# Moving two weight splits behind the last evacuations of the up-projection

## The reference, cut to what matters

```python
def conv_glu_ffn(h, w_up, conv_w, conv_b, w_down, rows):
    up = h @ w_up
    a, v = up[..., :D_FF], up[..., D_FF:]
    if rows is None:
        a = dwconv1d_centred(a, conv_w[FFN_CONV // 2])
    else:
        a = dwconv2d_grid(a, conv_w, rows)
    return (jax.nn.silu(a + conv_b) * v) @ w_down
```

## Time and profile before

| | us |
|---|---|
| median of three runs | 1760.85 |
| the profiled execution's own time | 1758.34 |
| its span | 1756.5 |
| PE busy in the span | 1613.1 |
| POOL busy | 909.2 |
| DVE busy | 900.9 |
| ACT busy | 709.4 |

### The profile page before, as it was taken

One profiled execution on the slowest core, in us unless ns is written; L12 is line 12 of the kernel. 1 busy time (PEld: TensorE's weight loads), 2 busy tenths in 40 slices (PEclk: granted clock), 3 DMA queues, 4 the chain that ended last, 5 costly groups with the idle time before them and its releaser, 6 DMA issues.

```text
span 1756.5 us, 31356 instructions
## 1 busy us (share of the span) xinstructions
PE 1613.1 (92%) x11787; PEld 1486.6 (85%) x11787; DVE 900.9 (51%) x1751; ACT 709.4 (40%) x1174; POOL 909.2 (52%) x516
## 2 busy tenths in 40 slices
PE   4999999999988999998799999988987969999995
PEld 2999987766977999997699899878787949999994
DVE  1533105655337777523733355778754256777423
ACT  2554432333324444333546453544434344444322
POOL 1455556566643555554345455777552524555551
PEclk9999999999998999999899999899878979999998
DMA  8334336786322333432223221000012313334320
GB/s 321 106 109 132 123 118 247 289 288 223 120 96 72 120 131 121 143 130 73 96 96 109 96 97 63 23 14 25 14 50 96 120 60 100 127 127 133 132 99 36
DMA packets 54967, 205.24 MB, mean 117 GB/s; under 512 B 6096, under 2 KB 6096, under 8 KB 54352
## 3 DMA queue, kind: packets, MB, share of 16 engines
q1 hardware_dynamic: 54864, 203.80, 34.1%
HBM read 196.44 MB, written 7.34 MB: 116 GB/s over the span
## 4 chain that ended last, share of the span: by engine, by line
PE 51%; issue 23%; POOL 12%; DVE 7%; DMA 4%; ACT 2%; POOLq 0%; SPq 0%; DVEq 0%; ACTq 0%
POOL wlo L287 12%; PE ps L325 5%; PE ps L327 5%; PE ps L326 5%; DMA raw<-w_ada_in 4%; PE ps L2308 4%; PE ps L2310 4%; PE ps L2309 4%; PE ps L770 3%; PE ps L772 3%; PE ps L771 3%; PE ps L367 1%; PE ps L1531 1%; PE ps L1429 1%; PE ps L1074 1%
## 5 line engine op out<-in xcount | busy, mean ns | idle before, releaser
L287 POOL TENSOR_TENSOR wlo<-raw,whi 128x1024 fp32r<-128x1024 f32 (+1 forms) x201 | 511.5, 2546 | 494.7 <-ACT whi L277 494.7
L277 ACT ACTIVATE whi<-raw 128x1024 fp32r<-128x1024 f32 (+1 forms) x250 | 274.9, 1101 | 600.5 <-PE ps L327 373.0
L325 PE MATMUL ps<-hhi,whi 128*128 128x384 f32 x704 | 239.1, 340 | 24.9 <-DVE hlo L432 24.9
L326 PE MATMUL ps<-hlo,whi 128*128 128x384 f32 x704 | 237.2, 337 | 0.0
L327 PE MATMUL ps<-hhi,wlo 128*128 128x384 f32 x704 | 237.1, 337 | 0.0
L609 DVE SCALAR_TENSOR_TENSOR evac<-ps,vec,evac 128x189 f32<-128x189 f32 (+3 forms) x440 | 166.6, 412 | 101.6 <-ACT evac L560 72.0
L2104 POOL TENSOR_TENSOR wlo<-raw,whi 128x1024 fp32r<-128x1024 f32 x49 | 118.2, 2412 | 143.8 <-ACT whi L277 143.8
L542 DVE SCALAR_TENSOR_TENSOR xr<-xr,evac 128x384 f32 x32 | 64.2, 2006 | 192.7 <-ACT evac L511 191.5
L325 PEld LDWEIGHTS ps<-hhi,whi 128*128 128x128 f32 x704 | 133.2, 189 | 30.7 <-issue 29.3
L2308 PE MATMUL ps<-hhi,whi 128*128 128x384 f32 x392 | 142.1, 363 | 13.0 <-DVE hlo L432 12.3
L770 PE MATMUL ps<-hhi,whi 128*128 128x384 f32 x392 | 133.3, 340 | 10.6 <-DVE hlo L432 10.0
(11 more groups left out here) (297 smaller groups left out, 3362.1 us busy)
## 6 DMA issues: line engine op xcount, KB each, us to landing
raw<-w_in_in SPq DMA_DIRECT2D x98, 512.0 KB, 3.5
raw<-w_ada_in SPq DMA_DIRECT2D x96, 512.0 KB, 5.1
raw<-w_up_in SPq DMA_DIRECT2D x88, 512.0 KB, 3.4
raw<-w_down_in SPq DMA_DIRECT2D x32, 704.0 KB, 4.1
raw<-w_out_in SPq DMA_DIRECT2D x32, 512.0 KB, 3.5
s<-s_ssd_in SPq DMA_DIRECT2D x8, 256.0 KB, 5.6
o_ssd_out<-st_sb SPq DMA_DIRECT2D x8, 256.0 KB, 2.7
S<-s_gdn_in SPq DMA_DIRECT2D x4, 512.0 KB, 3.4
```

Of the source, the lines that this page charges most:

```text
L277: act.activation(whi[:, s.mod(SPL), 0:p.kt * P], raw[:, b.mod(RAW), 0:p.kt * P], ACT.Copy).then_inc(hi_ready, 1)
L287: pool.tensor_tensor(wlo[:, s.mod(SPL), 0:p.kt * P], raw[:, b.mod(RAW), 0:p.kt * P], whi[:, s.mod(SPL), 0:p.kt * P].bitcast(F32), ALU.subt ...
L325: pe.matmul(out, a, rhi[:, r, :], start=(r == 0), stop=False)
L326: pe.matmul(out, a, rlo[:, lo_tile(r) if lo_tile else r, :], start=False, stop=False)
```

## The change

The two `split_hi` calls for the down-projection leave the last two steps of `up_act`. `up_act` now evacuates all 44 blocks and writes the last `hidden_hi`; only then `split_first` splits down blocks 0 and 1. It is called for both layers, so the change stands at two places of the program.

```diff
-            staggered(act, p, lambda j: split_hi(act, p, j), [(0, 1, tile_centre), (1, 2, silu), (2, p.n - 2, evacuate)])
-            for k in range(2):
-                split_hi(act, phase[f"down{lay}"], Idx(k))
-                evacuate(Idx(p.n - 2 + k))
+            staggered(act, p, lambda j: split_hi(act, p, j), [(0, 1, tile_centre), (1, 2, silu), (2, p.n, evacuate)])
             hidden_hi(Idx(FF_T - 1))
 
         def up_dve(dve, lay):
@@
                 modulate_hi(act, 2 * lay + 1)
                 up_act(act, lay)
+                split_first(act, f"down{lay}")
                 back_act(act, f"down{lay}", 2 * lay + 1)
```

## The result

Five runs of the changed kernel took 1771.06 to 1778.74 us, median 1773.51, against a median of 1760.06 us (1758.14 to 1765.07, five runs) of the kernel before. These two medians differ by 13.5 us. There are 27 runs of the changed kernel in all, 1771.06 to 1781.75 us, median 1775.9, which is 15.8 above 1760.06. The ratio of the two kernels is given as 1.0088, 95% interval 1.0073 to 1.0103: 15.5 us slower (12.8 to 18.2). Forecast were 17.5 us.

What follows compares the result with a forecast made beforehand. PE was taken as the bound of the down-projection, with nothing behind its first matmul to absorb delay. Relay 6.25 plus clock 2.5 gave 8.75 us a place, 17.5 for two; 1760.85 + 17.5 = 1778, range 1770 to 1784 us.

Steps and rivals of the forecast that it cites:

- The first split was covered by PE's last up block: Up-to-down passage, before the change: nearly the whole 1.38 us split of down block 0 lies under PE's up block 43.
- The relay: Up-to-down passage: tile 21's chain, then split, POOL and PE, starts the first down matmul 6.25 us later per place.
- The low part of tile 20 at 0.56: DVE, between taps and product: takes 0.56 us instead of 3.41, because POOL is idle until the moved split is done.
- The rival that prices it at 3.41: DVE's low part of tile 20 stays at 3.41 us from another cause than POOL: 1784 us; chance 0.05.
- The second split: Down block 1: its low part ends about 732.5, PE wants it at 735.0 or later; costs nothing, 2.5 us to spare.
- The clock: PE behind the new gap: 5.1 us at half clock, 45% lost, 2.3 us; 2.5 per place with 0.2 added.
- the 0.2 us that I added for the first matmul: First down matmul behind the gap: at half clock 0.2 us longer, an estimate, half of its 0.44 us.
- the middle of three rows from elsewhere: Half-clock time behind other gaps of the kernel before: 5.8, 5.1 and 4.4 us; 5.1 taken for the new gap.
- Loads: Down block 4's load is asked for 6.25 us later, lands about 733.5, needed past 746: costs nothing.
- what gets earlier: Tile 21's low part is ready at 725.22 instead of 729.17; PE reads it from 733.53, so no gain.
- The signs: Profile after: PE gap 6.9 us, half clock about 5 us, line 565 wait 0.6, POOL idle 8.4, no 3.41 at line 614.
- The sum: Both layers' places: 6.25 + 2.5 = 8.75 us each, 17.5 us together, giving a median of 1778 us.

Runs made afterwards that it cites:

- experiments 2: Kernel before, with only the down-projection's second split moved behind the last `hidden_hi`, the first left in place; ratio to before 1.0002 (0.9987 to 1.0017).
- experiment 3: Kernel before, with both splits moved one step later, behind `hidden_hi` of tile 20 but ahead of the last one; ratio to before 0.9998 (0.9987 to 1.0009).
- experiment 4: Kernel before, with both splits moved in layer 1 only; ratio to before 1.0045 (1.0031 to 1.0059), 7.9 us slower.
- experiment 1: Changed kernel plus 35 unused matmuls on PE between up- and down-projection of each layer; ratio to the kernel before 1.0054 (1.0039 to 1.0070).

## Why the prediction was right

- **The first split was covered by PE's last up block, and PE is the bound behind it.** Right. The delay at the start of down came out at its end in full. In the profiles of experiments 2 and 3 even waits of 1.8 and 0.9 us do so; their times do not resolve such sums.
- **The relay, 6.25 us a place.** Measured 6.14, and 6.13 in experiment 4. Link by link: the last `ghi` starts 1.71 us after PE's last up matmul ends (worked out: 1.75), the split 2.14 (2.18), POOL 3.58 (3.64), PE 6.79 (6.91).
- **The low part of tile 20 at 0.56.** Right, 0.55. In experiment 3, where POOL works at the same time, the same instruction took 1.47 us. In the kernel before, 42 of its 44 executions met POOL at work: 40 took 1.9 us and two 3.41, and each ended 0.41 to 0.42 us after POOL's instruction; the two with POOL idle took 0.56. The lock that the Trainium skill describes (SBUF — State Buffer, "SBUF: two separate sides") is what these traces show. The rival that prices it at 3.41 falls.
- **The second split costs nothing.** Right in the changed kernel: POOL made both low parts in one go (6.31 us for two), and PE had no second wait.
- **The clock, 2.5 us a place.** The mechanism was right and is shown by experiment 1. The size was a little high: 1.40 and 2.59 us, 4.0 instead of 5.0. I had taken 5.1 us at half clock from gaps elsewhere; it was 3.06 and 5.68 us, 4.4 on average. The share lost held: with starts 0.32 instead of 0.173 us apart it is 46%, and 3.06 x 0.46 = 1.4, 5.68 x 0.46 = 2.6. That is all of the loss, so the 0.2 us that I added for the first matmul were counted twice. Behind two equal gaps the half clock lasted 3.06 and 5.68 us; that the middle of three rows from elsewhere came within a microsecond of their average is luck.
- **Loads, and what gets earlier.** No wait of PE for either is in the trace after.
- **The signs.** The 0.32 us between starts, ACT's wait of 0.63 us at line 565, POOL's idle time of 8.34 us and the missing low part of 3.41 us are all there as foretold.
- **The sum.** 17.5 forecast, 16.3 at the places, 15.5 (12.8 to 18.2) in the runs. The time of 1778 was 4.5 above the median 1773.5; 1.2 of it are the terms, 0.8 is the median of before, which came out lower beside it, and the rest lies within the scatter of runs that spread over 7 us. Against the median of all 27 runs, 1775.9, the 1778 are 2.1 too high, and those two terms are nearly all of it.

What stays open: experiments 1, 2 and 3 each came out 2 to 3 us under the sum of their places, each at or just beyond the edge of its interval. In their profiles other stages moved by as much, with the clock (the sums of squares took 5.4 to 10.4 us in these traces). One pattern fits: the last norm's sum took 7.1 and 6.9 us in the traces of before and of experiment 3, and 5.43 in the six traces in which the places cost more. That would pay back 1.7 us, but with one trace of each kernel it is not shown. Whether a shift at the places helps those stages or the runs merely fell so was not settled. Nor was what decides whether a gap of 1.8 to 2.7 us brings the clock down.

## What to carry to other kernels

An instruction that feeds the busiest engine belongs in its queue at the moment its own input is free, ahead of anything that waits for a third engine; in an in-order queue the price of tidying it behind such a wait is the whole chain of that wait, here 6.1 us for a 1.4 us copy. A new idle stretch of PE can then be paid twice, once as length and once at half clock behind it. Here gaps of 4.7 and 6.8 us always were, one of 2.65 us once of two times, and those of 1.5 us not; where it happens, add the half-clock time times 0.46 for a dense stream. And where a wait of a few microseconds stands ahead of matmuls on the path, a few useless matmuls in it can pay: here -0.4%.

## What the runs showed of the hardware

- The same gap of 2.65 us in front of the same stream brought the granted clock down in one layer and not in the other; 4.7 and 6.8 us brought it down each time. Back at work without pause, PE stayed at half clock for 3.1 to 5.7 us in six cases, and the down-projection behind it lost 46% of that time in each: 1.4 us for 3.06, 1.6 for 3.41, 1.7 for 3.70, 2.4 for 5.24 and 2.6 for 5.68 (twice).
- Ahead of the squares of the layer norms, with the same code in eight traces, the clock fell at or behind a wait of 1.80 us in two of eight, of 2.26 us in six of eight and of 2.71 us in all sixteen.
- The down-projection's 128x384 matmuls (fp32r) start 0.32 us apart at 1.2 GHz and 0.173 us apart at 2.4 GHz, so full clock is worth a factor of 1.85, not 2. The plain float32 matmuls over the squares, in the changed kernel's first norm, start 0.64 us apart at 1.2 GHz and 0.32 at 2.4: there it is 2.
- A VectorE subtraction of two SBUF tiles that met POOL's at work ended 0.41 to 0.42 us after it in all 42 cases of the kernel before, and the trace shows that waiting as its duration (1.9 and 3.4 us instead of 0.56).
- With identical code ahead of it, one and the same point of the program was reached between 438.7 and 445.6 us.
